# Pool stage on raw x: the token scale goes into the band matrix, the channel scale into the eviction, and the pool products run by token tile

## The reference, cut to what matters

```python
POOL_WINDOWS = (2, 4, 8, 16)      # one per group of 256 channels
def rmsnorm(x, g):
    return x * rsqrt(mean(x * x, axis=-1) + EPS) * g
def pool_mixer(h, w, scale):
    for g, win in enumerate(POOL_WINDOWS):
        # mean over the last `win` tokens, less the token itself
        outs.append(window_sum / cnt - h[:, :, group g])
    y = einsum('btgc,gce->btge', stack(outs), w)   # 256x256 weights per group
    return y * scale
x = x + pool_mixer(rmsnorm(x, norm_mixer[0]), pool_w[0], pool_scale[0])
x = x + swiglu(rmsnorm(x, norm_ffn[0]), w_gate_up[0], w_down[0])
...
```

## Time and profile before

| | |
|---|---|
| runs, median (lowest to highest) | 1156.51 us (1156.18 to 1157.13) |
| the profiled execution: time, span of its trace | 1156.47 us, 1154.5 us |
| TensorE matmul busy | 1130.9 us, 98% of the span |
| VectorE, ScalarE, GpSimd busy | 778.6, 536.2, 32.9 us |
| mean granted clock of TensorE | 0.996 |

### The profile page before, as it was taken

How to read it: one execution, slowest core, us unless ns; L and a number is a source line. 1 busy time by engine, 2 the same in 40 slices (tenths; PEclk the granted TensorE clock), 3 DMA queues, 4 the chain that set the end, 5 groups by cost and what they waited for, 6 DMA issues and landing times. The chain is left out here.

```text
span 1154.5 us, 17146 instructions
## 1 busy us (share of the span) xinstructions
PE 1130.9 (98%) x6716; PEld 986.8 (85%) x6716; DVE 778.6 (67%) x998; ACT 536.2 (46%) x704; POOL 32.9 (3%) x47
## 2 busy tenths in 40 slices
PE   6999999999999999999999999999999999999997
PEld 5888888898888888879988888888899888888886
DVE  5766666846667666677576676666766766766665
ACT  5533433556654334444566443334446655343332
POOL 0000000000000000003000000000030000000000
PEclk9999999999999999999999999999999999999999
DMA  8765566664346555668423465556773234656550
GB/s 266 242 208 187 183 212 197 204 219 130 127 149 229 188 182 182 207 153 263 146 103 102 150 227 197 182 182 200 180 235 110 75 111 145 219 188 203 180 193 37
DMA packets 167132, 204.59 MB, mean 177 GB/s; under 512 B 19988, under 2 KB 150028, under 8 KB 167078
## 3 DMA queue, kind: packets, MB, share of 16 engines
q1 hardware_dynamic: 167078, 203.84, 55.0%
HBM read 202.66 MB, written 1.16 MB: 177 GB/s over the span
## 5 line engine op out<-in xcount | busy, mean ns | idle before, releaser
L633 ACT ACTIVATE whi<-raw 128x2048 fp32r<-128x2048 f32 x176 | 336.5, 1914 | 382.5 <-PE bank L1511 245.5
L945 DVE TENSOR_TENSOR wlo<-raw,whi 128x2048 fp32r<-128x2048 f32 x171 | 392.2, 2294 | 165.8 <-ACT whi L633 165.8
L1507 PE MATMUL bank<-h_both,whi 128*128 128x512 f32 x1280 | 304.6, 390 | 0.0
L1507 PEld LDWEIGHTS bank<-h_both,whi 128*128 128x128 f32 x1280 | 237.7, 188 | 47.7
L1481 PE MATMUL bank<-whi,o_hi 128*128 128x512 f32 x448 | 176.2, 393 | 0.6 <-DVE o_lo L1253 0.6
L1482 PE MATMUL bank<-wlo,o_hi 128*128 128x512 f32 x448 | 174.9, 390 | 0.0
L1483 PE MATMUL bank<-whi,o_lo 128*128 128x512 f32 x448 | 174.4, 389 | 0.0
L1511 PEld LDWEIGHTS bank<-h_both,wlo 128*128 128x128 f32 x1280 | 164.1, 191 | 6.2
L1511 PE MATMUL bank<-h_both,wlo 128*128 128x256 f32 x1280 | 166.0, 283 | 0.0
L1481 PEld LDWEIGHTS bank<-whi,o_hi 128*128 128x128 f32 x448 | 84.3, 188 | 18.3 <-issue 2.3
L1483 PEld LDWEIGHTS bank<-whi,o_lo 128*128 128x128 f32 x448 | 84.1, 188 | 18.0
(11 more groups left out here) (175 smaller groups left out, 1202.3 us busy)
## 6 DMA issues: line engine op xcount, KB each, us to landing
raw<-in_w_gate_up SPq DMA_DIRECT2D x44, 1024.0 KB, 5.1
raw<-in_w_down SPq DMA_DIRECT2D x44, 1024.0 KB, 4.9
raw<-in_w_gate SPq DMA_DIRECT2D x22, 1024.0 KB, 5.4
raw<-in_w_up SPq DMA_DIRECT2D x22, 1024.0 KB, 5.3
raw<-in_w_in SPq DMA_DIRECT2D x20, 1024.0 KB, 6.4
raw<-in_w_o SPq DMA_DIRECT2D x12, 1024.0 KB, 5.0
raw<-in_w_kv SPq DMA_DIRECT2D x8, 1024.0 KB, 5.6
raw<-in_w_q SPq DMA_DIRECT2D x4, 1024.0 KB, 5.4
```

The source lines that it names most:

```text
L633: act.activation(whi[:, s, :], raw[:, s, :], ACT.Copy).then_inc(hi_ready, 1)
L945: dve.tensor_tensor(wlo[:, s, :], raw[:, s, :], whi[:, s, :].bitcast(F32), ALU.subtract).then_inc(lo_ready, 1)
L1507: pe.matmul(bank[bk + jj][:, :], hi[:, kc, jj * P:(jj + 1) * P], h_both[:, kc, :, :].rearrange("p a t -> p (a t)"), start=(kc == 0), stop= ...
```

## The change

It does these things:

- The band's matmul reads x itself, not `xn`. The token scale `rstd` is multiplied into the band: VectorE writes two scaled copies of it, one for each token tile, by a tensor_scalar of 640 columns (`scaled_band`). `normalise(0, ...)`, four instructions of 512 columns, is gone.
- The band is stored once for both tiles (they share most of their columns), 160 columns per group in place of 272: 320 KB are loaded in place of 544 KB, and each partition's part is one piece.
- The channel gain is no longer copied to 128 partitions (512 KB). Eight rows of 128 floats (4 KB) are loaded, transposed on TensorE to one column for each chunk, and copied to `gcol` by ScalarE. The identity matrix is loaded early for that. The evictions apply the gain: ScalarE's copy with a scale operand, VectorE's as scalar_tensor_tensor, and so one for each chunk, 8 each of 256 columns, in place of 4 each of 512.
- The last of the four squares (tile 1, half 1) moves from ScalarE to VectorE.
- The split of the pool weights stands ahead of all evictions on both engines.
- The pool products run by token tile: outermost t, then h. The accumulators are banks 4 to 7 in this order. VectorE's scale and add follow: both halves of tile 0 first. `pool_scale(1, 1)` stands later, after the normalise of tile 0.
- The two one-hot matmuls and their tables become one, with 97 rows and 24 columns, which waits until bank 6 has been read (`pool_out`, 3). Two loads become one, two evictions one, and two stores one.

```diff
-BAND_W = 2 * P + 16
+BAND_W = P + 32
...
             for t in range(TT):
                 sp.dma_start(x[:, t, :], xv[t]).then_inc(x_in[t], 16)
-            load_gain(0)
-            sp.dma_start(band, c["c_band"].rearrange("g p n -> p g n")).then_inc(band_in, 16)
+            sp.dma_start(ident[:, :], c["c_ident"]).then_inc(ident_in, 16)
+            sp.dma_start(gain_rows, GAIN_SRC[0].rearrange("(k p) -> k p", p=P)).then_inc(gains_in[0], 16)
+            sp.dma_start(band, c["c_band"].rearrange("p g n -> p (g n)")).then_inc(band_in, 16)
...
-            sp.dma_start(ident[:, :], c["c_ident"]).then_inc(ident_in, 16)
...
-            for t in range(TT):
-                for h in range(2):
-                    square(0, t, h)
+            for t, h in ((0, 0), (0, 1), (1, 0)):
+                square(0, t, h, 2 if t else 1)
+            act.wait_ge(gain_turned, 1)
+            act.activation(gcol[:, :], bank[7][:, 0:KC], ACT.Copy).then_inc(gcol_ready, 1)
...
+            for part in range(2):
+                pool_whi(part)
+            act.wait_ge(gcol_ready, 1)
             for k in range(4):
-                if k % 2 == 0:
-                    pool_whi(k // 2)
                 act.wait_ge(pool_d, k + 1)
-                act.activation(h_hi[:, 2 * k:2 * k + 2, :], bank[k][:, :].rearrange("p (c k) -> p c k", c=2),
-                               ACT.Copy).then_inc(hT_hi, 1)
+                for c_ in (2 * k, 2 * k + 1):
+                    i = act.activation(h_hi[:, c_, :], bank[k][:, (c_ % 2) * T:(c_ % 2 + 1) * T], ACT.Copy, scale=gcol[:, c_:c_ + 1])
+                i.then_inc(hT_hi, 1)
...
                     pool_scale(0, 0)
-                    pool_scale(1, 0)
                     pool_add(0, 0)
                     pool_scale(0, 1)
                     pool_add(0, 1)
-                    pool_scale(1, 1)
+                    pool_scale(1, 0)
                     mean_square(1, 0)
                     normalise(1, 0, 0)
                     normalise(1, 0, 1)
                     pool_add(1, 0)
+                    pool_scale(1, 1)
+                    h_lo_out(1, 0, 0)
                     pool_add(1, 1)
-                    h_lo_out(1, 0, 0)
                     h_lo_out(1, 0, 1)
...
+            def scaled_band(t):
+
+                if t == 0:
+                    dve.wait_ge(band_in, 16)
+                dve.wait_ge(rstd_ready, t + 1)
+                dve.tensor_scalar(band_s[t], band, rstd[:, t:t + 1], None, ALU.mult).then_inc(xn_ready, 2)
 
             mean_square(0, 0)
-            normalise(0, 0, 0)
+            dve.wait_ge(x_in[1], 16)
+            dve.tensor_tensor_reduce(xn[:, 1, HALF:], x[:, 1, HALF:], x[:, 1, HALF:], 1.0 / D, 0.0, ALU.mult, ALU.add,
+                                     ssq[:, 1, 1:2]).then_inc(last_square, 1)
+            scaled_band(0)
+            dve.wait_ge(last_square, 1)
             mean_square(0, 1)
-            normalise(0, 0, 1)
-            for h in range(2):
-                normalise(0, 1, h)
+            scaled_band(1)
...
+            for part in range(2):
+                pool_wlo(part)
+            dve.wait_ge(gcol_ready, 1)
             for k in range(4):
-                if k % 2 == 0:
-                    pool_wlo(k // 2)
                 dve.wait_ge(hT_hi, k + 1)
-                dve.tensor_tensor(h_lo[:, 2 * k:2 * k + 2, :], bank[k][:, :].rearrange("p (c k) -> p c k", c=2),
-                                  h_hi[:, 2 * k:2 * k + 2, :].bitcast(F32), ALU.subtract).then_inc(hT_lo, 1)
+                for c_ in (2 * k, 2 * k + 1):
+                    i = dve.scalar_tensor_tensor(out=h_lo[:, c_, :], in0=bank[k][:, (c_ % 2) * T:(c_ % 2 + 1) * T],
+                                                 scalar=gcol[:, c_:c_ + 1], in1=h_hi[:, c_, :].bitcast(F32),
+                                                 op0=ALU.mult, op1=ALU.subtract)
+                i.then_inc(hT_lo, 1)
...
-            pe.wait_ge(band_in, 16)
+            pe.wait_ge(ident_in, 16)
+            pe.wait_ge(gains_in[0], 16)
+            pe.transpose(bank[7][:, 0:KC], gain_rows, ident[0:KC, 0:KC]).then_inc(gain_turned, 1)
...
             hi, lo = w8(POOL_U)
-            for h in range(2):
-                pe.wait_ge((pool_lo, lo_ready)[h], 1)
-                for t in range(TT):
+            for t in range(TT):
+                for h in range(2):
+                    pe.wait_ge((pool_lo, lo_ready)[h], 1)
                     for g in (2 * h, 2 * h + 1):
                         pe.wait_ge(hT_lo, g + 1)
                         for k in range(2):
-                            mm = three(bank[POOL_ACC[t][h]][:, (g % 2) * 256:(g % 2) * 256 + 256],
+                            mm = three(bank[ACC[2 * t + h]][:, (g % 2) * 256:(g % 2) * 256 + 256],
...
-            for i, lhs in enumerate((tab_moba[0:K, :], tab_t5[0:K, :])):
-                pe.matmul(bank[6 + i][0:lhs.shape[1], :], lhs, onehots[0:K, i, :], start=True, stop=True).then_inc(vec_done, 1)
+            pe.wait_ge(pool_out, 3)
+            pe.matmul(bank[6][0:24, :], tables[:, :], onehots, start=True, stop=True).then_inc(vec_done, 1)
```

More of the change, by code:

```diff
@@ L85, in shape_constants @@
     t = np.arange(T)
-    band = np.zeros((4, P, BAND_W), f)
+    band = np.zeros((P, 4, BAND_W), f)
     for g, win in enumerate((2, 4, 8, 16)):
@@ L91, in shape_constants @@
         full = np.where(inside, (f(1) / (t + 1 - start).astype(f))[None, :], f(0)) - np.eye(T, dtype=f)
-        band[g, :, 0:P + 16] = full[0:P, 0:P + 16]
-        band[g, :, P + 16:] = full[P:, P:]
+        band[:, g, 0:P + 16] = full[0:P, 0:P + 16]
+        band[:, g, P + 16:] = full[P:, P:P + 16]
     out["c_band"] = band
     d = np.arange(-(T - 1), T)
-    moba = np.zeros((NBUCKET + 1, SEQ_D), f)
+    onehots = np.zeros((T5_ROW + NBUCKET + 1, SEQ_D), f)
+    moba = onehots[0:NBUCKET + 1]
     past = d <= 0
@@ L108, in shape_constants @@
     t5[:, :d.size] = t5[:, :d.size][:, ::-1].copy()
-    out["c_t5"] = t5
+    out["c_onehots"] = onehots
     c = np.arange(64)
@@ L232, in bass_two_stacks @@
         wukv = sb("wukv", [P, 4, 2, HD])
-        band = qall[:, :, :].rearrange("p k t -> p (k t)")[:, 0:4 * BAND_W].rearrange("p (g n) -> p g n", g=4)
-        onehots = bias[:, 0:2 * SEQ_D].rearrange("p (i n) -> p i n", i=2)
-        vecs = bias[:, 2 * SEQ_D:4 * SEQ_D].rearrange("p (i n) -> p i n", i=2)
+        band_flat = qall[:, :, :].rearrange("p k t -> p (k t)")
+        band = band_flat[:, 0:4 * BAND_W]
+        band_s = [band_flat[:, (1 + i) * 4 * BAND_W:(2 + i) * 4 * BAND_W] for i in range(TT)]
+        gain_rows = xn[0:KC, 0, 0:P]
+        onehots = bias[0:T5_ROW + NBUCKET + 1, 0:SEQ_D]
+        vecs = bias[:, SEQ_D:2 * SEQ_D]
         pool_y = pr[:, 0:4, :, :].rearrange("p i a b -> p i (a b)")
@@ L633, in split, with square @@
                     act.activation(whi[:, s, :], raw[:, s, :], ACT.Copy).then_inc(hi_ready, 1)
-            def square(version, t, h):
+            def square(version, t, h, count=1):
                 if version:
@@ L673, in ffn @@
                 if f == 0:
[L674 to L676 removed]
+                    act.wait_ge(vec_done, 1)
+                    act.activation(vecs[0:24, :], bank[6][0:24, :], ACT.Copy).then_inc(vec_out, 1)
                 split(u0 + 2)
```

58 lines of the change are left out of this document (26 added, 32 removed).

## The result

| | before | after |
|---|---|---|
| median, us | 1156.22 (20 runs, 1155.32 to 1160.42) | 1158.57 (20 runs, 1157.17 to 1160.03) |
| profiled execution, us | 1156.47 | 1158.64 |
| its span, us | 1154.5 | 1156.6 |
| its mean granted clock | 0.996 | 0.995 |

The account below looks back on a forecast made before the run. TensorE, busy 98% of the span, was taken as the bound, with gains only in the first 35 us. Tile 1's transposes 3.5 us sooner plus 0.1 of closing slack gave 3.6 us: 1152.9 us, range 1151.0 to 1155.2.

Parts of the forecast that it names:

- The step that failed: Loads behind the start: one less issued, queue's data ends 1.8 us sooner; one-hot tables late by up to 0.4.
- Its last sign of being wrong: Forecast wrong if the first 35 us are won and lost again at a later idle row or low-clock stretch.
- The one on the slower side: Rival for the whole pool stage: clock stays low, costing 8.1 us in all, 1161.0 us; chance 0.05.
- Start: First band matmul: band lands at 7.3, scaling takes 0.55, so it starts at 7.85, 2.1 us sooner.
- upper bound of 8.07: Latest landing taken for the band's load: 8.07, where the larger third load landed before.
- The rate per KB: Loads behind x: 1056 KB took 4.46 us, 0.0042 us a KB; the new 388 KB take 1.6 us.
- GpSimd's power beside the reduce: Tile 0's power beside VectorE's reduce: done at 7.0, or 7.25 by the skill's rule, ahead of the band.
- The evictions: Band evictions, two instructions a bank on each engine: 0.8 us a bank, all banks in time, no stall.
- Second add: VectorE's last add for tile 0, after the second accumulator at 18.45: done at 19.8.
- its first rival: The clock doesn't fall: tile 1's transposes wait for `xn` until 28.8, 4.2 us sooner, 1152.1 us; chance 0.14.
- the forecast's own range: Range of the 1152.9 us forecast from band bounds and evictions: 1151.7 to 1154.1 us; chance 0.58.
- order: Tile 0's transposes: 1.6 us sooner from product order, shorter one-hot stage and 0.84 us idle that mostly goes.

Follow-up runs that it names:

- 96 and 1 rows: Changed kernel with the one-hot load cut in two, 96 rows and 1 row, in place of one of 97: 1153.59 us, 0.997 to the kernel before.
- the version with the band first: 96-and-1-row version with the band's load ahead of identity and gains, gains' transpose between the two tiles' passes: 1153.79 us; again on another chip, 1153.32.
- matmul moved: Changed kernel, load of 97 rows kept, with the one-hot matmul moved behind the transposes of tile 1: 1154.61 us, 0.9973 to the kernel before.
- old order: 96-and-1-row version with the pool products by feature half outermost again, accumulators and VectorE's order as before: 1154.86 us, 0.9982 to the kernel before.
- that one run: Kernel before with only the one-hot merge: one table of 97 rows, one load, one matmul, one eviction: 1161.28 us, 1.0039 to the kernel before.

## Why the prediction was wrong, point by point

- **The step that failed** is the place of the one-hot load: "The loads behind it move along: one less is issued, the queue's data ends 1.8 us sooner" and, for the matmul, "If its tables land late, by up to 0.4 as I read their place at the end of the small loads, the transposes slip to 22.7". I sized this load by its bytes and its place in the queue, and took the merge of two loads for a saving of one issue. What counted was the number of its rows: 97, one behind the other, 8.1 us, where a load of 96 and 1, of 98 or of 128 rows is ready when TensorE comes. The wait was 4.7 us, not 0 to 0.4. The prediction priced the merged matmul (1.0 for 1.9 us) and never the shape of the merged load. No row of the kernel before shows a load of 97 rows, but the Trainium skill has the rule ("DMA: Bandwidth & Descriptors", section "Why a DMA increments its semaphore by 16 and not by 1"), and the step should have been bounded by it.
- **The load's consumer was on the path.** The prediction did name the right queue: the transposes stand behind the one-hot matmul. It asked what happens if the tables are a little late, and no rival asked what happens if they are very late. Its last sign of being wrong, the first 35 us won and lost again at an idle row, is what came.
- **Of the rivals none came true in the changed kernel.** The one on the slower side, with 1161.0 and a chance of 0.05, let the clock stay low through the products; that the result is on its side doesn't bear it out. The clock was up through all products (the last ones 0.12 us apart at 21.5) and fell only once TensorE had no work.
- **Start**, forecast at 7.85, measured 8.68, and 8.79 with 96 and 1 rows: 0.8 to 0.9 undersized. The band landed at 2.55 + 5.4 = 7.95, not at 7.3, and in the nine traces with this load order at 7.65 to 8.55, in four of them above the upper bound of 8.07 too:

```profile
qall<-in_c_band SPq DMA_DIRECT2D x1, 320.0 KB, 5.4
```

  The rate per KB, taken from large rows, didn't hold for what stood ahead of it. In the version with the band first, its load took 5.5 us from 1.66, and 5.1 in the second trace: there it lands at 7.16 and 6.76, on the mean 1.1 us sooner than behind the identity and the gains' rows (6.96 against 8.11), where the rate of the prediction (0.0042 us a KB) gives 0.3 for their 68 KB. But behind them the band is also issued 0.89 us later (2.55 in place of 1.66); how much of the 1.1 us is the small pieces and how much the later issue was not tested.
- **`scaled_band`** 0.55, as taken. **GpSimd's power beside the reduce** took 0.93 where it takes 0.55 alone, and ended at 7.26, where the prediction had 7.0 and, by the rule of the Trainium skill (SBUF — State Buffer, "SBUF: two separate sides"), 7.25. The trace agrees with the rule in that the power ends 0.42 us behind the reduce (6.16 + 0.68 = 6.84), as it ended 0.41 behind the normalise in the kernel before (9.61 and 10.02). That the two times nearly meet is luck: the reduce ran 0.14 later than the 6.7 taken, and a full 0.55 behind it would be 7.39. It cost nothing as long as the band came later; with the band first it became the bound.

```profile
6.33 0.93 POOL L588 TENSOR_TENSOR rstd<-msq,neghalf 128x1 f32<-128x1 f32 x1 [5.19 <-DVE msq L966]
```

- **The evictions** were taken as 0.8 us a bank on either engine, without a stall: 3.46 and 3.41 for four banks are 0.86, and no idle row stands between the products. Right.
- **Products** 15.97 to 21.96, forecast 15.55 to 21.35. **Second add** from 19.95 and done at 20.64, forecast done at 19.8. **`xn`** 22.37, forecast 21.6. Each late by the 0.4 to 0.8 of the start; the steps between are right.
- **Behind the wait** the forecast can be read on the version with 96 and 1 rows: transposes of tile 0 at 23.29 (forecast 22.6), of tile 1 at 29.62 (forecast 29.5), 3.45 us before the kernel before (forecast 3.5). That the sum comes out so near is in part luck: a start 0.9 late, and a clock that did not fall, which the prediction had as its first rival (TensorE then "waits for `xn` until 28.8": it does wait, 0.56 us, and 28.8 with the late start comes near the 29.62 measured). Of the 3.45 us, 3.14 are left at the end of the program, 0.3 go at a wait for VectorE at 44, and the medians beside the kernel before give 2.8 and 3.2. This version's time, 1153.59, lies inside the forecast's own range of 1151.7 to 1154.1.

So the mechanisms of the main parts were right (start: 3 us of lateness arrive; order: 1.3 of the 1.6 us that it was put at together with the one-hot stage), and one small edit, which was counted at next to nothing, cost more than all of them won (4.9 us against 2.7).

## What to carry to other kernels

When loads are merged or a table is resized, look at the count of rows (the outermost dimension) of the new transfer before its bytes: 97 rows, a prime, went one behind the other here, and a split into 96 and 1 or one row of padding took the wait away. An edit that costs nothing by its instructions still has to be bounded by the latest moment at which its data may land, above all where it stands in an in-order queue ahead of work on the path. And where a change of several parts comes out wrong, run the version before with the smallest part alone; here that one run showed which part of the change held the loss.

## What the runs showed of the hardware

- Loads of 97 and 127 rows of 2 KB go row behind row at 84 ns, 24.4 GB/s; 97 rows take 8.1 us, 127 rows some 10.7 (127 times 84 ns). Loads of 96, 98 and 128 rows had landed when TensorE came, at 22.1 to 23.0 us.
- The same load, in the same order, landed 5.1 to 6.0 us after its issue in nine traces, and the same 48 band passes took 7.16 to 8.21 us.
- GpSimd's power on one column takes 0.55 us alone and 0.93 to 0.99 when it starts beside a VectorE instruction of 512 columns with two inputs, and ends 0.4 us behind that instruction.
- TensorE's granted clock fell to 0.50 while the engine stood idle for 4.7 us and not where it did other work in that time. It didn't fall for idle pieces of 1.22 and 0.55 us (matmul moved), but the sixteen matmuls behind one of 1.59 us took 5.50 us (old order), and those of the kernel before behind 0.84 and 0.18 us as well. The length of the idle piece alone doesn't tell; what else has a part in it wasn't tried.
